# A first projection fed tile by tile: loads, squares and weight halves in order of first use

## What is computed

```python
def project(x, norm_g, w_in, w_a2, b_a2, q_g, k_g):
    xn = rmsnorm(x, norm_g)                       # x * rsqrt(mean(x*x)+eps) * gain
    proj = xn @ w_in                              # 1024 -> 3088 columns
    gq, gk, gv, gate, alr, sq, sk, sv = split(proj)
    log_a = log_sigmoid(alr @ w_a2 + b_a2) / 16
    ...
# then: gated linear attention in chunks of 64 (gq, gk, gv, log_a),
#       stick-breaking attention (sq, sk, sv) with the cache,
#       x + mix @ w_out, and a squared-ReLU MLP of width 4096
```

## Time and profile before

| what | value |
|---|---|
| median of three runs | 3177.38 us |
| lowest, highest | 3176.07, 3178.87 us |
| the profiled execution's own time | 3173.07 us |
| its span | 3171.3 us |
| busy: PE, DVE, ACT, POOL | 97%, 60%, 53%, 35% |
| mean granted TensorE clock | 0.986 |
| moved by DMA | 400.66 MB |

### The profile page before, as it was taken

The page is one execution under the profiler, slowest core; times in us unless marked ns, Lnnn a source line. Parts: engine busy times, 40 slices in busy tenths (PEclk is TensorE's granted clock), DMA queues, the critical chain, the costliest instruction groups (busy, mean ns, idle before and its releaser), DMA issues. The chain is left out here.

```text
span 3171.3 us, 48786 instructions
## 1 busy us (share of the span) xinstructions
PE 3076.5 (97%) x18258; PEld 2640.2 (83%) x18258; DVE 1893.9 (60%) x3388; ACT 1693.8 (53%) x3148; POOL 1107.1 (35%) x642
## 2 busy tenths in 40 slices
PE   6999999999779999999999999999999999999999
PEld 5887788877679989888888988888898888889998
DVE  2565646546446666566665776777757667653333
ACT  3443434443357766555555666666556655543443
POOL 0331513215135663333333232222333333334665
PEclk9999999999779999999999999999999999999999
DMA  4654645544455554323333323222233333333443
GB/s 148 185 176 140 193 132 161 155 138 114 147 156 176 182 177 128 113 86 104 101 91 115 107 97 99 91 92 89 81 126 115 133 98 102 98 99 120 133 145 111
DMA packets 310747, 400.66 MB, mean 126 GB/s; under 512 B 70433, under 2 KB 225074, under 8 KB 309490
## 3 DMA queue, kind: packets, MB, share of 16 engines
q1 hardware_dynamic: 310514, 397.55, 40.1%
HBM read 339.95 MB, written 57.54 MB: 125 GB/s over the span
## 5 line engine op out<-in xcount | busy, mean ns | idle before, releaser
L1861 POOL TENSOR_TENSOR st_ul<-st_ur,st_uh 128x1024 fp32r<-128x1024 f32 x180 | 428.8, 2404 | 803.4 <-ACT st_uh L1669 803.4
L1868 POOL TENSOR_TENSOR st_dl<-st_dr,st_dh 128x1024 fp32r<-128x1024 f32 x180 | 430.9, 2415 | 610.4 <-ACT st_dh L1679 610.4
L1835 DVE TENSOR_TENSOR st_ya<-st_ya,st_dp 128x512 f32<-128x512 f32 x544 | 368.6, 681 | 97.2 <-PE st_dp L1589 96.0
L1636 ACT ACTIVATE st_a<-st_z 128x512 f32<-128x512 f32 (+3 forms) x336 | 177.2, 527 | 380.9 <-PE st_z L1448 252.7
L1761 DVE TENSOR_TENSOR_SCAN st_g<-st_z,st_g,st_a 128x511 f32<-128x511 f32 (+3 forms) x336 | 371.0, 1104 | 15.6 <-DVE st_g L1754 0.5
L1822 DVE TENSOR_TENSOR st_tl<-st_dp,st_th 128x512 fp32r<-128x512 f32 (+2 forms) x168 | 96.8, 576 | 437.6 <-ACT st_dp L1717 437.5
L1589 PE MATMUL st_dp<-st_dh,st_th 128*128 128x512 f32 x1020 | 336.9, 402 | 0.7 <-DVE st_ya L1835 0.6
L1589 PE MATMUL st_dp<-st_dh,st_tl 128*128 128x512 f32 x1020 | 336.9, 401 | 0.0
L1589 PE MATMUL st_dp<-st_dl,st_th 128*128 128x512 f32 x1020 | 334.5, 399 | 0.0
L1471 PEld LDWEIGHTS st_po<-st_v,st_wt 128*128 128x128 f32 x2256 | 303.3, 194 | 36.2 <-DMA st_v<-out_new_v 7.6
L495 PE MATMUL fr_pj<-fr_wl,fr_xh 128*128 128x512 f32 x816 | 330.3, 405 | 0.0
(11 more groups left out here) (165 smaller groups left out, 5738.6 us busy)
## 6 DMA issues: line engine op xcount, KB each, us to landing
st_ur<-in_w_up SPq DMA_DIRECT2D x75, 1024.0 KB, 5.3
st_dr<-in_w_down SPq DMA_DIRECT2D x75, 1024.0 KB, 4.9
fr_wr<-in_w_in SPq DMA_DIRECT2D x96, 512.0 KB, 4.0
st_ur<-in_w_out SPq DMA_DIRECT2D x10, 1024.0 KB, 5.0
st_dr<-in_w_out SPq DMA_DIRECT2D x10, 1024.0 KB, 5.0
fr_xb<-in_x SPq DMA_DIRECT2D x17, 512.0 KB, 4.5
st_ya<-in_x SPq DMA_DIRECT2D x17, 512.0 KB, 7.3
out_y<-st_ya SPq DMA_DIRECT2D x16, 512.0 KB, 3.9
```

What stands on the lines that cost most here:

```text
L1835: dve.tensor_tensor(part, part, dp[:, k % BANKS], ALU.add).then_inc(s_fd, 1)
L1861: pool.tensor_tensor(ul[:, c], ur[:, c], raw(uh[:, c]), ALU.subtract).then_inc(s_ul, 1)
L1868: pool.tensor_tensor(dl[:, k], dr[:, k], raw(dh[:, k]), ALU.subtract).then_inc(s_dl, 1)
```

## The change

Nothing is computed otherwise, and no instruction is added or taken away. Four things change: the keys of the first block's x transposes, which become -4500, 3000, 8400 and 13800 (tile 0 before slot 0, tiles 1, 2 and 3 inside slots 0, 1 and 2); the keys of the first four weight pairs on ACT and DVE, now -5000 to 500; the first loads on SP, in order of first use; and the ring `wr`, which has four places in place of two, so that every weight load after the first four is issued two pairs earlier than before.

```diff
 NC = PAST // P
 W_RING = 5
+WR = 4
...
         tt = []
         for b in range(NB):
             for j in range(NTS[b]):
-                if b == 0 and j < 3:
-                    at = -30e3 + 3e3 * j
+                if b == 0:
+                    at = (-4.5e3, 3e3, 8.4e3, 13.8e3)[j]
                 elif j < 3:
                     at = self.end(b - 1, SB_V, j + 1) + 20
                 else:
...
     def split(self, m):
         q, i = m // PAIRS, m % PAIRS
         if q == 0:
-            return -36e3 + 100 * i
+            return (-5e3, -3.2e3, -1.5e3, 500.0)[i]
         n = self.number[q // NG, q % NG, 0] - 1
         return n * SLOT + i * SLOT / PAIRS + 50 if i else n * SLOT - 2000
 
...
         ssx = m.sb("ssx", [P, 3, 3])
-        wr = m.sb("wr", [P, 2, 2, 512])
+        wr = m.sb("wr", [P, WR, 2, 512])
         wh = m.sb("wh", [P, W_RING, 2, 512], F32R)
         wl = m.sb("wl", [P, W_RING, 2, 512], F32R)
         wah = m.sb("wah", [P, KC * RANK + P - RANK], F32R)
...
-        s_wr, s_wh, s_wl, s_wf = m.sems("wr", 2), m.sem("wh"), m.sem("wl"), m.sem("wf")
+        s_wr, s_wh, s_wl, s_wf = m.sems("wr", WR), m.sem("wh"), m.sem("wl"), m.sem("wf")
...
         @block.sync
         def _(sp):
             sp.dma_start(idt[:], ident).then_inc(s_c, 16)
-            sp.dma_start(gb[:], bcast_rows(norm_g, D)).then_inc(s_c, 16)
+
+            def gains():
+                yield -91.5e3
+                sp.dma_start(gb[:], bcast_rows(norm_g, D)).then_inc(s_c, 16)
 
             def x_loads():
                 for t in range(TILES):
                     at = x_at(t) - 30e3
                     if t >= 3:
                         at = max(at, x_at(t - 3) + 100)
-                    yield -90e3 + t if t < 3 else at
+                    yield -92e3 + 3e3 * t if t < 3 else at
                     if t >= 3:
                         sp.wait_ge(s_tt, plan.tt.full("x", *tiles[t - 3], 1))
                     sp.dma_start(xb[:, t % 3], rows(x, t)).then_inc(s_x[t % 3], 16)
 
             def constants():
-                yield -89e3
+                yield -85e3
                 sp.wait_ge(s_cs, 2)
                 sp.dma_start(lt[:, 0, 0:KC * RANK].rearrange("p (c n) -> p c n", n=RANK),
                              w_in[:, C_ALR:C_ALR + RANK].rearrange("(c p) n -> p c n", p=P)).then_inc(s_wa, 16)
...
             def w_loads():
                 for k in range(NW):
                     q, i = k // PAIRS, k % PAIRS
-                    yield -88.5e3 + k if k < 2 else plan.split(k - 2) + 200
-                    if k >= 2:
-                        sp.wait_ge(s_wl, k - 1)
+                    yield (-91e3, -90e3, -88e3, -87e3)[k] if k < WR else plan.split(k - WR) + 200
+                    if k >= WR:
+                        sp.wait_ge(s_wl, k - WR + 1)
                     g = q % NG
-                    sp.dma_start(wr[:, k % 2], w_in[i * 2 * P:(i + 1) * 2 * P, GROUP_COLS[g]:GROUP_COLS[g] + 512]
-                                 .rearrange("(c p) n -> p c n", p=P)).then_inc(s_wr[k % 2], 16)
+                    sp.dma_start(wr[:, k % WR], w_in[i * 2 * P:(i + 1) * 2 * P, GROUP_COLS[g]:GROUP_COLS[g] + 512]
+                                 .rearrange("(c p) n -> p c n", p=P)).then_inc(s_wr[k % WR], 16)
 
             def cache_loads():
                 for t in range(NC):
...
-            Streams(x_loads(), constants(), w_loads(), cache_loads(), log_a_stores(), kept_stores(), key_stores(),
+            Streams(gains(), x_loads(), constants(), w_loads(), cache_loads(), log_a_stores(), kept_stores(), key_stores(),
                     transposed_stores(), gla_loads(), gate_loads(), mix_stores(), states()).to(1e12)
...
             act.preload_act_table_set("natural_log_exp_and_others")
 
             def constants():
-                yield -70e3
+                yield 5600.0
                 act.wait_ge(s_wa, 16)
                 act.activation(wah[:, 0:KC * RANK], war, ACT.Copy).then_inc(s_wah, 1)
                 yield 9000.0
...
 
             def squares():
                 for t, (b, j) in enumerate(tiles):
-                    yield x_at(t) - 9000
+                    yield x_at(t) - (6000 if t in (1, 2) else 9000)
                     act.wait_ge(s_x[t % 3], 16 * (t // 3 + 1))
                     if b:
                         act.wait_ge(s_pjd, plan.pj.freed(b - 1, G_GATE, NTS[b - 1] - 1))
...
             def splits():
                 for k in range(NW):
                     yield plan.split(k)
-                    act.wait_ge(s_wr[k % 2], 16 * (k // 2 + 1))
+                    act.wait_ge(s_wr[k % WR], 16 * (k // WR + 1))
                     if k >= W_RING:
                         pair_done(k - W_RING)
-                    act.activation(wh[:, k % W_RING], wr[:, k % 2], ACT.Copy).then_inc(s_wh, 1)
+                    act.activation(wh[:, k % W_RING], wr[:, k % WR], ACT.Copy).then_inc(s_wh, 1)
 
             def pair_done(k):
                 q, i = k // PAIRS, k % PAIRS
...
             dve.wait_ge(s_c, 32)
 
             def alr_halves():
-                yield -69e3
+                yield 6200.0
                 dve.wait_ge(s_wah, 1)
                 dve.wait_ge(s_cs, 3)
                 dve.tensor_tensor(wal[:, 0:KC * RANK], war, raw(wah[:, 0:KC * RANK]), ALU.subtract).then_inc(s_wal, 1)
...
                 for k in range(NW):
                     yield plan.split(k) + 100
                     dve.wait_ge(s_wh, k + 1)
-                    dve.tensor_tensor(wl[:, k % W_RING], wr[:, k % 2], raw(wh[:, k % W_RING]), ALU.subtract).then_inc(s_wl, 1)
+                    dve.tensor_tensor(wl[:, k % W_RING], wr[:, k % WR], raw(wh[:, k % W_RING]), ALU.subtract).then_inc(s_wl, 1)
 
             def ranks():
                 for b in range(NB):
...
 
             def inverse_rms():
                 for t in range(TILES):
-                    yield x_at(t) - 7500
+                    yield x_at(t) - (5500 if t in (1, 2) else 7500)
                     pool.wait_ge(s_sq, t + 1)
                     pool.tensor_scalar(ssx[:, t % 3, 1:2], ssx[:, t % 3, 0:1], 1.0 / D, EPS, ALU.mult, ALU.add).then_inc(s_r1, 1)
                     pool.wait_ge(s_r1, t + 1)
```

## The result

| | before | after |
|---|---|---|
| median of the runs | 3177.2 us | 3158.81 us |
| lowest, highest | 3176.07, 3178.87 us | 3155.16, 3159.81 us |
| the profiled execution's own time, span | 3173.07, 3171.3 us | 3159.41, 3157.6 us |

The ratio is 0.994, with a 95% interval of 0.9922 to 0.9957: 18.4 us faster. The forecast was 3164.4 with a range down to 3159.5, so the sign was right and the size too small. Two later comparisons gave 0.9938 (0.9924 to 0.9952) and 0.9947 (0.9934 to 0.9961). Two executions of the kernel before in the later comparisons were in a slower state (4328.73 and 4918.16 us) and are left out of the medians and ratios here.

What follows compares the result with a forecast made beforehand. TensorE, busy 97% of the span, was taken as the bound after an idle start-up. Slot 3 starting at 36.55 instead of 49.75 us gives 13 us, all else 0: 3177.4 - 13 = 3164.4 us, range 3159.5 to 3170.5.

Steps and rivals of the forecast that it cites:

- The sum: Slot 3's first matmul moves from 49.75 to 36.55 us; the 13.2 us, taken as 13, are the whole gain.
- the ring of four: Weight loads after the head: ACT's 70.2 us of waits nearly vanish, but TensorE gains 0, within 3 us either side.
- Loads and the first chain: Start-up: tile 0 lands at 6.0 us, the gain at 7.4, first transpose at 9.7, loads 1.45 us apart per 512 KB.
- Slot 0: First slot matmul at 13.1 us in place of 31.83, with stops inside the slot; slot 1 starts at 22.0.
- The stop for the third pair's rest: Inside slot 0: DVE does this rest from 15.7 to 16.9 us, so the 13th matmul waits until 16.9.
- The new wait: Before slot 3, TensorE stands 2.0 us for tile 3's rests, behind the fifth pair's rest on DVE; bounds 0 and 3.5.
- 2 us in hand: Gated attention's constants, due on ACT at about 28 us: their copies have this slack before tile 3's; otherwise up to 1 us.
- The slow matmuls behind the stop: After the wait before slot 3: lost clock was only a bound, bringing that wait to about 3.5 us.
- The slow head: Start-up: low clock through slot 0 (gain 9.9 us, 3167.5) or GpSimd not ready until 12.16 (gain 8.4, 3169); chance 0.20.
- a first call's hidden cost: GpSimd at start-up: some 6 us without visible instruction, over by about 7.6 us if run from the last memset, costing nothing.
- Given back later: First stage's end hangs on gated attention or stores: 7 us or more return before 848 us, 3171 to 3178; chance 0.07.
- The slower case: Late weight loads stop TensorE once in each of 23 later groups; at 1.0 us per stop 3187 us; chance 0.03.

Runs made afterwards that it cites:

- ring_only: The kernel before with only the weight ring raised from two to four places; 3162.52 us, ratio 0.9964 to the kernel before.
- order_only: The changed kernel with the weight ring back at two places, all else kept; 3161.95 us, ratio 0.9958 to the kernel before.
- after_ab: The changed kernel without any edit, timed again beside the later edits; 3158.6 us, ratio 0.9947 to the kernel before.
- after_aa: The changed kernel without any edit, timed again against the kernel before; 3154.74 us, ratio 0.9938.
- before_aa: The kernel before, unchanged, timed against itself; 3172.71 us, ratio 0.9998.
- loads_only: The changed kernel with the transposes of x tiles 1 and 2 ahead of slot 0 again; 3165.26 us, ratio 0.9975 to the kernel before.
- ring_again: Second trace of the kernel before with four ring places; slot 3 at 44.74 us, last scan at 817.6 us, no run time given.
- order_again: Second trace of the changed kernel with two ring places; slot 3 at 36.19 us, last scan at 813.4 us, no run time given.

## Why the prediction was right in its place and short in its size

**The sum.** The forecast took all the gain from slot 3's start, 13 us. That term came out at 12.93, in part by luck: tile 3's transposes came 1.3 us ahead of the forecast, and slot 3 began 6.92 us after them and not 5.35, so that two errors cancelled. In the changed kernel's traces it is then worth less at once and more later, which the sum had both at nothing.

**The step that failed: the ring of four.** The prediction counted 0 for it "since TensorE never waited for a weight rest there". The premise is true and the conclusion isn't: TensorE waited for other work of VectorE, and once of ScalarE, that stood, in order, behind a rest or copy whose load was late. In place of 0 the term measures 5.4 us over thirteen traces, with ring_only and order_only showing it from both sides. The bound of 3 us to either side was too narrow as well. With the 5.4 us added, the forecast of 13 would have been 18.4, the measured difference of the medians; that it fits to the tenth is chance, given what stays open below. The row that had it was the earlier trace rows, where 70.2 us of waits stand on an engine that is nobody's bottleneck; which of them were passed on could be read only by following each to what stands behind it.

**Loads and the first chain.** Tile 0 landed at 4.7 us, at the lower bound of 4.8 and not at 6.0. The scaling then waited for the gain, at 7.0 where 7.4 was counted, and the transposes came at 8.55 where 9.7 was forecast. ScalarE's rows show the first pair copied from 8.75 and tile 2 squared from 15.68 (8.9 and 16.1 forecast). Five loads of 512 KB landed from the one to the other, 1.39 us apart, where 1.45 was counted.

**Slot 0.** Forecast 13.1 for its start, 22.0 for slot 1; measured 12.31 and 20.6. The stop for the third pair's rest didn't come, since that rest began at 14.09, not 15.7, and TensorE's first nine matmuls were slow:

```profile
14.09 1.23 DVE L800 TENSOR_TENSOR fr_wl<-fr_wr,fr_wh 128x1024 fp32r<-128x1024 f32 x1 [0.69 <-ACT fr_wh L651]
...
16.42 1.22 DVE L800 TENSOR_TENSOR fr_wl<-fr_wr,fr_wh 128x1024 fp32r<-128x1024 f32 x1
```

**The new wait.** Its place was right, and its cause in part; the 2.0 us were 3.37, 2.22 and 3.80 in the three traces of the changed kernel. The other part is ScalarE's wait for constants, which the prediction had given "2 us in hand". They were due at 25.5, not at 28, and landed at 30.7. On SP they stand behind the eighth pair's load, the last of the three in the second row here, which waits for the fourth pair's rest (16.42 + 1.22 = 17.64):

```profile
6.32 5.51 SPq L350 DMA_DIRECT2D fr_wa<-in_w_a  x1
...
14.10 3.94 SPq L368 DMA_DIRECT2D fr_wr<-in_w_in  x3
...
19.57 1.95 SPq L359 DMA_DIRECT2D fr_og<-in_gla_norm_g  x4
```

Issued from 19.57 on, at a DMA share near 1, they took 7.2 us in the median to land, and the last one over 9. The long issue in the first row (5.51 us for 16 KB) didn't set this: it was over at 11.83, and the queue had to wait for VectorE's rests until 17.64 in any case. How far it delayed the loads in between isn't shown. The head's gain of 1.3 us over the forecast (tile 3's transposes at 29.90, not 31.2) went into this stop. The slow matmuls behind the stop, named only as a bound, cost another 1.5 us in this trace, 2.6 behind the stop of 3.80, and nothing behind the stop of 2.22.

**Rivals.** The slow head fell: GpSimd began at 6.05, on the heel of the square, so nothing but the square had kept it until 12.16 before.

```profile
6.05 0.19 POOL L967 TENSOR_SCALAR fr_ssx<-fr_ssx 128x1 f32<-128x1 f32 x1 [4.41 <-ACT fr_ge L633]
```

The prediction's estimate from the Trainium skill (GPSIMD Engine Reference, Instruction dispatch), that a first call's hidden cost might end at about 7.6 us, is not borne out by this row: the first call after the memsets began at 6.05, 0.18 us behind the end of the square, and took 0.19. The slow matmuls of slot 0 were nine here, seven in after_ab and fourteen in after_aa, which cost about 1 us more than nine; never the whole slot. Given back later: 2.8 us, as the next paragraph says, and not 7. The slower case, a TensorE stop per group from late weight loads, is refuted by the same rows that show the opposite.

**What stays open.** By the means of the traces, before reaches `st_dp` at 899.5 us and after at 884.7: 14.8 us, of which 11.2 at the latent matmul and 6.4 up to the scan, less 2.8 given back at the border of the stages (St is 73.2 to 73.3 against 69.5 and 71.4). The medians of the three comparisons say 15.7, 18.4 and 18.6 us. From `st_dp` to the end the same program takes 2268.1 to 2274.1 us in thirteen traces, without order by kernel, so one trace can't decide 3 us. Whether the 2.8 us belong to the two parts together or to chance isn't settled; the longer wait for the v store lies in it, and what would lengthen that is not shown.

## What to carry to other kernels

An engine's wait is free only if nothing that the bottleneck needs stands behind it in order: follow each long wait through the queues of the engines in between, not just to its own consumer. Read a transfer's landing as issue plus time to landing, and order the loads and the engines' programs together, since here the new order of the loads without that of the transposes gained nothing over the deeper ring alone (slot 3 at 45.60 against 43.72 and 44.74), and with it slot 3 came at 36.82. Take a stop apart with one edit for each part, compare it with a trace in which TensorE arrives at the same time, and price it by the next matmuls' spacing too: a listed idle of 1.13 us cost 1.58.

## What was not expected of the hardware

- At the start of slot 0 the changed kernel was slow (0.43 us from start to start) for seven, nine and fourteen matmuls in its three traces. With 24 transposes ahead, full pace (0.23) came at once in before_aa and ring_only, and from the third to the fifth matmul in loads_only, before and ring_again.
- Behind stops of 3.37 and 3.80 us matmuls of 128x256 took 1.91 us for eight; behind 1.64 (twice) and 2.22 us they took 1.09 to 1.11; behind 1.80 us the first eight took 1.10, the next 1.72 and 1.91.
- One issue of 16 KB held SP for 5.40 to 5.81 us in the seven traces that have eight loads of 512 KB ahead of it, issued in some 4.6 us; with six of them ahead (order_only, order_again) it took 0.68 and 0.78, and the 1 KB issue behind it 3.17 and 3.02.
